# Opening of a two-layer transformer pass: first weight chunk in halves ahead of the inputs, one share of a low part moved to VectorE, table scaling moved to ScalarE

## The reference, cut to what matters

```python
h = x
hn = rms_norm(h, norm_mix_g[0])
proj = hn @ ab_w_in[0]
qa, ka, va, qb, kb, vb = jnp.split(proj, split_ab, axis=-1)
qa = rms_norm(qa.reshape(b, s, A_HEADS, HEAD_DIM), a_q_norm_g[0])   # ka likewise
...                                      # rotary tables cos, sin applied to qa and ka
o_a = gqa_attention(qa, ka, va)          # scale HEAD_DIM ** -0.5 = 0.125
o_b = dilated_attention(qb, kb, vb, rel_bias)
h = h + jnp.concatenate([o_a, o_b], -1) @ ab_w_out[0]
```

## Time and profile before

| What | Value |
|---|---|
| device time, median of 3 runs | 1393.79 us (1391.31 to 1403.01) |
| the profiled execution's own time | 1391.83 us |
| its span in the profile | 1390.0 us |
| TensorE busy | 1285.0 us, 92% of the span |
| GpSimd busy | 954.3 us, 69% |
| ScalarE busy | 674.1 us, 48% |
| VectorE busy | 540.9 us, 39% |
| DMA | 204.58 MB, 147 GB/s on average |
| TensorE's granted clock, mean | 0.962 |

### The profile page before, as it was taken

How to read it: one execution, slowest core, us unless ns; L and a number is a source line. 1 busy time by engine, 2 the same in 40 slices (tenths; PEclk the granted TensorE clock), 3 DMA queues, 4 the chain that set the end, 5 groups by cost and what they waited for, 6 DMA issues and landing times.

```text
span 1390.0 us, 23576 instructions
## 1 busy us (share of the span) xinstructions
PE 1285.0 (92%) x9496; PEld 1195.0 (86%) x9496; DVE 540.9 (39%) x933; ACT 674.1 (48%) x918; POOL 954.3 (69%) x748
## 2 busy tenths in 40 slices
PE   4998999999888999999999987999996996999996
PEld 3874999999865999999978566999996885999995
DVE  2476322110564222101625345444225456544304
ACT  4344555443445655343554235666436553766532
POOL 4860598979830888888777234888893853788890
PEclk9999999999989999999999798999997998999998
DMA  6570255555420455545543212555552432355540
GB/s 242 196 213 0 92 186 185 194 174 173 177 94 1 152 182 182 199 165 185 178 170 124 80 33 89 183 182 182 183 182 91 152 121 91 124 183 184 179 152 31
DMA packets 31033, 204.58 MB, mean 147 GB/s; under 512 B 3368, under 2 KB 5544, under 8 KB 6872
## 3 DMA queue, kind: packets, MB, share of 16 engines
q1 hardware_dynamic: 28192, 199.22, 40.8%
q10 hardware_dynamic: 2744, 3.95, 1.0%
HBM read 202.09 MB, written 1.59 MB: 147 GB/s over the span
## 4 chain that ended last, share of the span: by engine, by line
POOL 52%; issue 27%; PE 18%; DVE 2%; ACT 1%; DMA 0%; POOLq 0%; DVEq 0%; SPq 0%; ACTq 0%
POOL w_lo L1858 52%; PE bank L266 6%; PE bank L267 5%; PE bank L268 5%; DMA raw<-stream 0%; ACT w_hi L801 0%; DVE rstd L1226 0%; POOLq L1855 0%; PE bank L434 0%; DVE yb_down L1231 0%; PE bank L399 0%; DVE yb_down L1230 0%; PE bank L723 0%; ACT h L871 0%; PE bank L712 0%
## 5 line engine op out<-in xcount | busy, mean ns | idle before, releaser
L1858 POOL TENSOR_TENSOR w_lo<-raw,w_hi 128x512 fp32r<-128x512 f32 x744 | 954.1, 1321 | 403.1 <-ACT w_hi L801 403.0
L266 PE MATMUL bank<-xs_hi,w_hi 128*128 128x256 f32 x1712 | 495.3, 289 | 45.2 <-DVE xs_lo L1207 23.3
L267 PE MATMUL bank<-xs_lo,w_hi 128*128 128x256 f32 x1712 | 490.6, 287 | 0.0
L268 PE MATMUL bank<-xs_hi,w_lo 128*128 128x256 f32 x1712 | 490.2, 286 | 0.0
L801 ACT ACTIVATE w_hi<-raw 128x2048 fp32r<-128x2048 f32 x186 | 354.5, 1914 | 210.0 <-PE bank L268 174.5
L266 PEld LDWEIGHTS bank<-xs_hi,w_hi 128*128 128x128 f32 x1712 | 335.2, 196 | 51.7 <-issue 45.5
L267 PEld LDWEIGHTS bank<-xs_lo,w_hi 128*128 128x128 f32 x1712 | 335.5, 196 | 0.5 <-issue 0.2
L268 PEld LDWEIGHTS bank<-xs_hi,w_lo 128*128 128x128 f32 x1712 | 335.0, 196 | 0.0
L266 PE MATMUL bank<-hT_hi,w_hi 128*128 128x256 f32 x1096 | 311.9, 285 | 12.8 <-DVE arena L1551 5.7
L268 PE MATMUL bank<-hT_hi,w_lo 128*128 128x256 f32 x1096 | 311.7, 284 | 0.0
L267 PE MATMUL bank<-hT_lo,w_hi 128*128 128x256 f32 x864 | 244.4, 283 | 0.0
(11 more groups left out here) (302 smaller groups left out, 1188.7 us busy)
## 6 DMA issues: line engine op xcount, KB each, us to landing
raw<-stream SPq DMA_DIRECT2D x186, 1024.0 KB, 4.8
arena<-vec_scratch ACTq DMA_DIRECT2D x8, 256.0 KB, 7.4
con<-consts SPq DMA_DIRECT2D x1, 1288.0 KB
h<-x SPq DMA_DIRECT2D x1, 1024.0 KB, 4.9
out<-h SPq DMA_DIRECT2D x4, 256.0 KB, 2.1
con<-pool_mat ACTq DMA_DIRECT2D x1, 768.0 KB, 9.7
vec_scratch<-vec_row ACTq DMA_DIRECT2D x1, 512.0 KB
arena<-evb_row ACTq DMA_DIRECT2D x1, 512.0 KB, 8.1
```

The lines of the kernel that those rows point to most:

```text
L266: mm(out, lh, rh, start=start, stop=False, skip_group_check=True)
L267: mm(out, lh, rl, start=False, stop=False, skip_group_check=True)
L268: return mm(out, ll, rh, start=False, stop=stop, skip_group_check=True)
L1858: ins = nc.gpsimd.tensor_tensor(w_lo[:, slot_c].rearrange("p a b -> p (a b)")[:, part], raw[:, slot_r, part], w_hi[:, slot_c].rearrange("p ...
```

## The change

1. SyncE's queue: the first half of chunk 0 comes first, then only the 8 gain columns of the parameters, the first quarter of `x`, the second half of chunk 0, the other three quarters of `x`, chunk 1, then the constants, the rest of the parameters, chunk 2 and the rest. The first 12 passes of its loop are written out; the reload of chunk 1's buffer waits for VectorE's share too.
2. ScalarE rounds chunk 0 in two halves with pair 0 between them, rounds chunk 1 before the squares, and writes the four rotary tables (behind `cut(5)`).
3. GpSimd does the low part of chunk 0 as 2 + 2 pieces with a signal after each two, and only the first two pieces of chunk 1. Its first 12 chunks are written out.
4. VectorE does the second half of chunk 1's low part (128 x 1024) behind its eight low parts and ahead of the adds, scales two gain columns by 0.125, and later waits for the tables instead of writing them.
5. TensorE starts when the low part of chunk 0's first half is there, and waits for the second half at tile 4.

```diff
             def chunk(c):
-                pe.wait_ge(S("w_lo_ready"), c + 1)
+                if c == 1:
+                    pe.wait_ge(S("w_lo_second"), 1)
+                if c > 0:
+                    pe.wait_ge(S("w_lo_ready"), c + 1)
...
+                        if c == 0 and j == 0 and k in (0, 4):
+                            pe.wait_ge(S("w_lo_first" if k == 0 else "w_lo_ready"), 1)
...
-            cut(0)
-            act.wait_ge(S("x_loaded"), 16)
+            def cut_half(n):
+                act.wait_ge(S(("raw_first", "raw0")[n]), 16)
+                af(w_hi[:, 0].rearrange("p a b -> p (a b)")[:, n * CW // 2:(n + 1) * CW // 2],
+                   raw[:, 0, n * CW // 2:(n + 1) * CW // 2], ACT.Copy).then_inc(S(("w_hi_first", "w_hi_ready")[n]), 1)
+            cut_half(0)
+            act.wait_ge(S("gain_loaded"), 16)
+            for n in range(4):
+                act.wait_ge(S(f"x_loaded{n}"), 16)
+                high_pair(n, pair_of_h(n), ("mix_g", 0))
+                if n == 0:
+                    cut_half(1)
+            cut(1)
             act.wait_ge(S("base_loaded"), 32)
-            for n in range(4):
-                high_pair(n, pair_of_h(n), ("mix_g", 0))
...
-            for c in range(1, AHEAD):
+            for c in range(2, AHEAD):
                 cut(c)
...
+            act.wait_ge(S("gains_scaled"), 1)
+            for tab, table, g in zip(tabs, ("cosA", "sinA") * 2, (small[:, 62:63], small[:, 63:64], pc("ak_g"), pc("ak_gs"))):
+                af(tab, cc(table, T), ACT.Copy, scale=g).then_inc(S("tables_ready"), 1)
...
+            link(v.memset(small[:, :], 0.0))
+            dve.wait_ge(S("gain_loaded"), 16)
+            for n in range(4):
+                dve.wait_ge(S(f"x_loaded{n}"), 16)
+                low_pair(n, h[:, 2 * n:2 * n + 2, :].rearrange("p a b -> p (a b)"), ("mix_g", 0))
+            dve.wait_ge(S("w_hi_ready"), 2)
+            half = slice(CW // 2, CW)
+            v.tensor_tensor(w_lo[:, 1].rearrange("p a b -> p (a b)")[:, half], raw[:, 1, half],
+                            w_hi[:, 1].rearrange("p a b -> p (a b)")[:, half].bitcast(F32), ALU.subtract)\
+                .then_inc(S("w_lo_second"), 1)
             dve.wait_ge(S("base_loaded"), 32)
...
+            v.tensor_scalar(small[:, 62:64], par[:, a_gain], 0.125, None, ALU.mult).then_inc(S("gains_scaled"), 1)
...
-            link(v.tensor_scalar(tabs[0], cc("cosA", T), pc("aq_g"), 0.125, ALU.mult, ALU.mult))
...
+            dve.wait_ge(S("tables_ready"), 4)
...
-            sp.dma_start(h[:, :, :], x).then_inc(S("x_loaded"), 16)
+            sp.dma_start(raw[:, 0, 0:CW // 2], stream[0][:, 0:CW // 2]).then_inc(S("raw_first"), 16)
+            g = slice(COL["mix_g"], COL["mix_g"] + 8)
+            sp.dma_start(par[:, g], params[:, g]).then_inc(S("gain_loaded"), 16)
+            sp.dma_start(h[:, 0:2, :], x[:, 0:2, :]).then_inc(S("x_loaded0"), 16)
+            sp.dma_start(raw[:, 0, CW // 2:CW], stream[0][:, CW // 2:CW]).then_inc(S("raw0"), 16)
+            for n in range(1, 4):
+                sp.dma_start(h[:, 2 * n:2 * n + 2, :], x[:, 2 * n:2 * n + 2, :]).then_inc(S(f"x_loaded{n}"), 16)
+            sp.dma_start(raw[:, 1, :], stream[1]).then_inc(S("raw1"), 16)
...
+            for c in range(RAW, RAW + body):
+                if c == RAW + 1:
+                    sp.wait_ge(S("w_lo_second"), 1)
+                sp.wait_ge(S("w_lo_ready"), c - RAW + 1)
+                sp.dma_start(raw[:, c % RAW, :], stream[c]).then_inc(S(f"raw{c % RAW}"), 16)
```

More of the change, by code:

```diff
@@ L134, in build @@
         lg = carve(1024, "p (b n) -> p b n", b=2)
+        tabs = [lg[:, 0, 0:T], lg[:, 0, T:2 * T], lg[:, 1, 0:T], lg[:, 1, T:2 * T]]
         qstd = [sq[:, 2 * n:2 * n + 2, :].rearrange("p a b -> p (a b)") for n in range(3)]
@@ L1430, in hb2 @@
                 return HT2[name]
+            link(v.memset(small[:, :], 0.0))
[8 more added lines that the diff above has]
+                .then_inc(S("w_lo_second"), 1)
             dve.wait_ge(S("base_loaded"), 32)
-            link(v.memset(small[:, :], 0.0))
-            for n in range(4):
-                low_pair(n, h[:, 2 * n:2 * n + 2, :].rearrange("p a b -> p (a b)"), ("mix_g", 0))
+            a_gain = slice(COL["aq_g"], COL["aq_g"] + 2)
+            v.tensor_scalar(small[:, 62:64], par[:, a_gain], 0.125, None, ALU.mult).then_inc(S("gains_scaled"), 1)
             for n in range(1, 4):
@@ L1853, in _, with low @@
         def _(pool):
-            def low(c, slot_r, slot_c):
+            def low(c, slot_r, slot_c, pieces=range(PIECES)):
                 pool.wait_ge(S("w_hi_ready"), c + 1)
-                for q in range(PIECES):
+                for q in pieces:
                     part = slice(q * CW // PIECES, (q + 1) * CW // PIECES)
@@ L1860, in low @@
                         w_hi[:, slot_c].rearrange("p a b -> p (a b)")[:, part].bitcast(F32), ALU.subtract)
-                ins.then_inc(S("w_lo_ready"), 1)
+                return ins
+            pool.wait_ge(S("w_hi_first"), 1)
+            for q in range(PIECES // 2):
+                part = slice(q * CW // PIECES, (q + 1) * CW // PIECES)
+                ins = nc.gpsimd.tensor_tensor(
+                    w_lo[:, 0].rearrange("p a b -> p (a b)")[:, part], raw[:, 0, part],
+                    w_hi[:, 0].rearrange("p a b -> p (a b)")[:, part].bitcast(F32), ALU.subtract)
@@ L1863, in _ @@
+            ins.then_inc(S("w_lo_first"), 1)
+            low(0, 0, 0, range(PIECES // 2, PIECES)).then_inc(S("w_lo_ready"), 1)
+            low(1, 1, 1, range(PIECES // 2)).then_inc(S("w_lo_ready"), 1)
             body = RAW * CUT
-            with nc.gpsimd.Fori(0, CHUNKS // body) as i:
+            for c in range(2, body):
+                low(c, c % RAW, c % CUT).then_inc(S("w_lo_ready"), 1)
+            with nc.gpsimd.Fori(0, CHUNKS // body - 1) as i:
                 for j in range(body):
-                    low(i * body + j, j % RAW, j % CUT)
+                    low(i * body + (j + body), j % RAW, j % CUT).then_inc(S("w_lo_ready"), 1)
@@ L1876, in _ @@
-            for c in range(RAW):
-                sp.dma_start(raw[:, c, :], stream[c]).then_inc(S(f"raw{c}"), 16)
+            sp.dma_start(par[:, g.stop:NPAR], params[:, g.stop:NPAR]).then_inc(S("base_loaded"), 16)
+            sp.dma_start(raw[:, 2, :], stream[2]).then_inc(S("raw2"), 16)
             sp.dma_start(con[:, 256:NCON], consts[:, 256:NCON]).then_inc(S("const_loaded"), 16)
```

16 lines of the change are left out of this document (6 added, 10 removed).

## The result

| What | Before | After |
|---|---|---|
| median of the paired runs | 1397.49 us (20 runs) | 1389.82 us (20 runs, 1380.45 to 1400.31) |
| ratio, 95% interval | | 0.9948 (0.9925 to 0.997) |
| profiled execution's own time | 1391.83 | 1395.84 |
| span; mean granted clock | 1390.0; 0.962 | 1394.1; 0.957 |

The change gains about 0.5%, some 8 us, where the prediction said 1380.0 (1376.5 to 1384.5). The profiled execution of after is longer than that of before, so two spans must not be subtracted here. The start has to be read by its own marks.

A forecast was written before the change was run, and what follows sets the result against it. The start was taken as bound by getting the first operands ready, the rest by TensorE. Chunk 2's first matmul at 16.8 + 2.9 + 5.7 = 25.4 instead of 38.5 saves 13.1 us: 1380.0 us, range 1376.5 to 1384.5.

The forecast's parts named there:

- Counting back: Loads at the start: usable at 9.49 - (2.51 - B) / 0.42 us for B MB; chunk 1 at 11.0, taken as 11.2.
- TensorE on chunk 0: First chunk's matmuls: 20 slow at 0.213 us, 28 fast at 0.12, 7.6 us from 8.7, ending at 16.5.
- turns: Low parts: VectorE gets in between two GpSimd pieces, costing GpSimd about 0.2 us per 256 columns; chunk 1 takes 2.5 + 1.0.
- the marker: Chunk 2's first matmul on TensorE, forecast to move from 38.50 to 25.4 us, with TensorE hardly stopping behind it.
- The base: Whole kernel's starting time: profiled 1391.83 us gives 1378.7, median 1393.79 gives 1380.7; 1380.0 was put.
- Removing them gives nothing: Rotary tables on VectorE: they stood in front of an 8.80 us idle stretch, so taking them away gains nothing.
- Tables on ScalarE hidden: Rotary tables behind `cut(5)`: they cost ScalarE 1.6 us, covered by 4.6 us of slack before TensorE needs the squares.
- Chunk 2 tie: Start of chunk 2: its low part from GpSimd and TensorE are both ready at 25.4 us, so any delay shows.
- The first one: Rival at the start: slow small rows, turns or slow clock make chunk 0 or 1 late; 1382 to 1384 us, 17%.
- The second: Rival behind chunk 2's first matmul: GpSimd or VectorE becomes the bound, 3 or 4 chunks lose 1.2 us each; 1384 to 1385, 8%.
- the fourth: Rival in attention from about 78 us: TensorE's clock falls later for longer; 40 us more would give 1397.6 us; 3%.
- Rival 5: Rival on chunk 0: quarters of `x` hold TensorE, start at 11.5 us, chunk 1 still decides; 1381 to 1383 us, 5%.

The follow-up runs named there:

- big_rows: The changed kernel with chunk 0 and `x` each loaded whole by one DMA; 1384.37 us, ratio 0.99, and when repeated 1387.37 us, ratio 0.9934.
- tables_on_dve: The changed kernel with the four rotary tables written by VectorE again, at the old place; 1405.77 us.
- tables_third: The same kernel as tables_on_dve, executed a third time; no total time given, its four tables took 0.84, 1.27, 1.27 and 1.26 us.
- after_again: The changed kernel run once more, unedited; 1388.54 us, ratio 0.9934 to the kernel before.

## Why the prediction was wrong

The time came out 9.8 us over the forecast (1389.8 against 1380.0), and above the range. By its own steps:

- **The step that failed: the loads.** "Counting back" at 0.42 MB per us, with 0.2 us for short rows, put chunk 1 at 11.2 and the range's worst end at 12.2. It was 14.6, and never under 12.7 in nine profiles of these loads. The mechanism (the load holds chunk 1's rounding) was right, the term was off by 3.4 us, by two halves: the cuts moved 0.7 MB less than before's loads by 8 us (250 to 258 GB/s against 291 to 434), and 0.7 MB more of the later loads overtook chunk 1, where "counting back" allows 0.4 MB as in before. big_rows, with 1 MB loads, shows neither: 10.7. The row taken as the worst (303) came from small rows between large loads; no row of before showed several DMAs of 256 to 512 KB in a line, so its 1.0 us was no bound. The Trainium skill (DMA: Bandwidth & Descriptors, Measured) advises 1 MiB or more for each DMA and names 341 GB/s for one, measured on GpSimd's queue; here, on SyncE's, such loads reached 420 and the smaller ones 254, so its direction agrees.
- **A second term failed beside it: TensorE on chunk 0.** The prediction put its end at 16.5. In after it was 20.1: the start 0.8 later and the wait for pair 1 1.1 longer (both from the late quarters), and 34 slow matmuls instead of 20 (14 x 0.093 = 1.3). In the nine profiles of these loads the last matmul on chunk 0 started at 17.1 to 20.5, in big_rows at 17.5, never as early as forecast. In three of the nine (after, tables_on_dve, tables_third) TensorE had no idle time ahead of chunk 1. With chunk 0 ending as in these profiles, chunk 1 could not have begun before 17.2, even if it had been ready at 16.8. How long the slow pace lasts differs in one kernel (18.14 in after, 13.58 in after_again); why stays open.
- **From chunk 1's load on, the steps held.** ScalarE 1.91, turns 3.57 against 3.6, then 8.62 us to the marker against 2.9 + 5.7. Marker 28.93 = 25.4 + 3.5. First matmul 9.47 against 8.7: the late quarter 0 cost 2.0 us, of which 1.2 were covered by GpSimd's two pieces.
- **The base.** From the three runs' median of 1393.79 and the profiled 1391.83 I took about 1393.1. In the 20 paired runs the kernel before stands at 1397.49. That is 4.4 us of the miss, and says nothing about the change. Three runs of a kernel that spreads over 17 us could not tell it better; the range didn't hold this. Neither miss leaves the range alone: the marker's 3.5 us alone give 1383.5, the base alone 1384.4.
- **The rest, 1.9 us**: 13.1 - 3.5 = 9.6 at the marks, 7.7 in the medians. Over all 116 fast runs of before on record (mean 1397.9) and 31 of after (1389.1) the difference is 8.7, with a standard error of about 1.1, so 9.6 is within it. Two things differ from execution to execution behind va, the half clock and the long wait; that they differ between the two kernels isn't shown.
- **"Removing them gives nothing" was wrong**, without effect on the sum. At the old place, with GpSimd started late, two of the four tables took 1.26 us and TensorE didn't feel it. With the start moved forward, GpSimd runs without a pause past them, and in two of four executions VectorE stands still for 14 us. The table step adds nothing to the 9.6; in such executions it keeps it from being lost. The prediction priced VectorE's side of the sharing by turns alone.
- **Tables on ScalarE hidden: right.** They ran from 35.44 to 37.1 and the squares of `qa` ended at 38.5, well ahead of TensorE's need at 43.3 (52.90 less 9.6).
- **Chunk 2 tie: right, in part by luck.** GpSimd started on it at 23.60, so it was done near 28.6, 0.3 us ahead of the marker. Two errors cancel in it: VectorE's subtraction ended 1.3 us behind chunk 1's rounding, not 2.4, and the 2-column instruction, put at 0.15 at most, took 1.25.
- **Rivals.** The first one came: chunk 1 late by small things. It named slow small rows as one source and priced all at 2 to 4 us, and the marker lost 3.5; its time, 1382 to 1384, missed by the base. The slow clock that it named lasted too, and was covered by chunk 1's lateness. The second and the fourth did not: no new gap between chunks 2 and 6, and no half-clock stretch of after before 86.6; the mean granted clock is 0.959 over 31 runs of after and 0.958 over 96 of before. Rival 5's quarters do hold TensorE (both waits on chunk 0 are for `xs_lo`), and it was right that chunk 1 decides anyway, though in after chunk 0 ends at the same time.

## What to carry to other kernels

Price a load by the size of the DMA that brings it: cutting the first megabytes into quarters to start earlier cost more at the next chunk than it won at the first (va 1.9 us later than with whole loads). And count what TensorE itself needs on the first chunk: it can end as late as the load that one watches. Before engine work is called hidden, ask whether the engine beside it will still have pauses after the change: VectorE lives in GpSimd's pauses here, and filling them cost 2 us in one place and up to 9 us in another. One execution is not enough to say that they share well: the same instruction took 0.73 or 10.65 us. When executions spread as these do, take the gain from marks early in the trace and the base from many runs, not from three.
